# GpSimd sums the attention weights of a query tile before TensorE adds them over the keys

## The reference

```python
s = jnp.einsum('bhtd,bhsd->bhts', q, k) * w_intra
num = w_inter[..., None] * jnp.einsum('bhvk,bhtk->bhtv', C, q) + jnp.einsum('bhts,bhsv->bhtv', s, v)
den = w_inter * jnp.einsum('bhk,bhtk->bht', n, q) + jnp.sum(s, axis=-1)
h = num / jnp.maximum(jnp.abs(den), jnp.exp(-m_t))[..., None]
```

## Time and profile before

| | us |
|---|---|
| median of 3 runs | 1104.81 (1104.47 to 1109.66) |
| profiled execution | 1102.33 |
| its span | 1100.6 |
| VectorE busy | 452.7 |
| ScalarE busy | 254.4 |
| GpSimd busy | 155.4 |

### The profile page before, as it was taken

The page is one execution under the profiler, slowest core; times in us unless marked ns, Lnnn a source line. Parts: engine busy times, 40 slices in busy tenths (PEclk is TensorE's granted clock), DMA queues, the critical chain, the costliest instruction groups (busy, mean ns, idle before and its releaser), DMA issues.

```text
span 1100.6 us, 12588 instructions
## 1 busy us (share of the span) xinstructions
PE 1077.2 (98%) x4688; PEld 702.4 (64%) x4688; DVE 452.7 (41%) x1075; ACT 254.4 (23%) x525; POOL 155.4 (14%) x240
## 2 busy tenths in 40 slices
PE   7999999999999999999999999999999999999997
PEld 5777777777765354453634677777766666656667
DVE  7433243333347577575665100005243333343215
ACT  3211111111235323232331000010123333242221
POOL 5200010000110324113232011011110101000100
PEclk9999999999999999999999999999999999999999
DMA  6323223322346997979979322122211101202202
GB/s 256 106 82 130 86 81 129 128 81 106 111 144 248 337 372 286 339 278 354 368 303 329 151 75 76 38 77 99 87 54 45 60 20 60 94 17 101 72 24 97
DMA packets 44637, 162.26 MB, mean 147 GB/s; under 512 B 4844, under 2 KB 9196, under 8 KB 35632
## 3 DMA queue, kind: packets, MB, share of 16 engines
q1 hardware_dynamic: 44592, 161.65, 40.5%
HBM read 104.42 MB, written 57.21 MB: 147 GB/s over the span
## 4 chain that ended last, share of the span: by engine, by line
PE 91%; DVE 5%; DMA 2%; ACT 1%; issue 1%; POOL 0%; SPq 0%; DVEq 0%; ACTq 0%; POOLq 0%
PE work_b L633 27%; PE work_a L633 23%; PE work_b L1077 5%; PE work_a L896 5%; PE work_a L790 4%; PE bank L681 3%; PE bank L863 2%; PE work_b L846 2%; DVE arena L1890 2%; PE work_a L1147 2%; PE bank L1122 2%; PE bank L1252 1%; PE work_a L1107 1%; PE work_a L872 1%; PE bank L1125 1%; PE work_a L1220 1%
## 5 line engine op out<-in xcount | busy, mean ns | idle before, releaser
L633 PE MATMUL work_b<-arena,ring 128*128 128x320 f32 x832 | 230.5, 433 | 0.0
L633 PEld LDWEIGHTS work_b<-arena,ring 128*128 128x128 f32 x832 | 155.6, 190 | 61.0
L633 PE MATMUL work_a<-arena,ring 128*128 128x320 f32 x640 | 177.7, 436 | 6.7 <-DMA ring<-in_stream 6.7
L633 PEld LDWEIGHTS work_a<-arena,ring 128*128 128x128 f32 x640 | 121.6, 192 | 55.7 <-DMA ring<-in_stream 6.7
L1890 DVE SCALAR_TENSOR_TENSOR arena<-arena,bank 128x512 f32<-128x512 f32 x128 | 87.1, 743 | 65.1 <-PE bank L863 65.1
L1711 DVE COPY arena<-bank 128x384 f32<-128x384 f32 x64 | 28.5, 486 | 130.1 <-PE bank L681 130.0
L633 PE MATMUL work_a<-xc,ring 128*128 128x320 f32 x256 | 70.4, 434 | 1.9 <-ACT arena L1423 1.3
L633 PE MATMUL work_b<-xc,ring 128*128 128x320 f32 x256 | 69.6, 432 | 0.0
L896 PE MATMUL work_a<-arena 128*128 128x512 f32 x128 | 64.4, 615 | 2.8 <-ACT arena L1405 2.8
L633 PEld LDWEIGHTS work_a<-xc,ring 128*128 128x128 f32 x256 | 48.3, 190 | 23.6 <-ACT arena L1423 2.1
L633 PEld LDWEIGHTS work_b<-xc,ring 128*128 128x128 f32 x256 | 48.6, 190 | 20.3
(11 more groups left out here) (289 smaller groups left out, 1342.2 us busy)
## 6 DMA issues: line engine op xcount, KB each, us to landing
ring<-in_stream SPq DMA_DIRECT2D x66, 512.0 KB, 3.5
arena<-in_c SPq DMA_DIRECT2D x32, 1024.0 KB, 8.2
out_s_c<-arena SPq DMA_DIRECT2D x32, 1024.0 KB, 5.6
v_scratch<-arena SPq DMA_DIRECT2D x16, 320.0 KB, 4.7
k_scratch<-arena SPq DMA_DIRECT2D x16, 320.0 KB, 4.4
z_scratch<-arena SPq DMA_DIRECT2D x16, 320.0 KB, 4.6
arena<-k_scratch SPq DMA_DIRECT2D x4, 1280.0 KB, 12.9
arena<-z_scratch SPq DMA_DIRECT2D x4, 1280.0 KB, 9.8
```

The source lines that it names most:

```text
L633: done = mm(halves(buf)[:, a, :], lhs, rhs[:, a * HALF:(a + 1) * HALF], start=first, stop=last)
```

## The change

A new SBUF buffer ptsum of 512 columns holds the sums over key tiles. Behind the product of key tile s (s = 1 to 3), GpSimd adds tile s of pt to what it has for the query tiles s to 3: first tile 0 plus tile 1 (384 columns), then plus tile 2 (256), then plus tile 3 (128). After the addition s, the block of query tile s is complete. It waits for the addition before, and for VectorE's product, and raises weights_summed. The three additions stand at the head of GpSimd's work for a head, ahead of inverse_root(h, 0).

TensorE's sums are then one matmul for each query tile: tile 0 straight from pt, tiles 1 to 3 from ptsum, and the streams' as before. All five stand in small_sums, in each head; the scores have none between them any more. The semaphore's declaration is left out here.

```diff
--- before.py
+++ after.py
...
@@ -310,6 +310,7 @@
         hn = [take(HD) for _ in range(2)]
         cps = [take(HD) for _ in range(2)]
         kwsum = take(KH, P)
+        ptsum = take(SEQ)
         st6, mv = take(TT, 6), take(TT, 2)
         tiny = take(TT, 8)
         den_s = take(16)
@@ -768,9 +769,9 @@
             def weights_of(s, t):
                 return pt[:, OFF[s] + (t - s) * P:OFF[s] + (t - s + 1) * P]
 
-            def key_sum(s, t):
-                mm(small[:, S_DEN + t:S_DEN + t + 1], weights_of(s, t), ones_f[:, 0:1],
-                   start=s == keys_of(t)[0], stop=s == keys_of(t)[-1], skip_group_check=True)
+            def key_sum(t):
+                lhs = ptsum[:, t * P:(t + 1) * P] if 0 < t < NP else weights_of(t, t)
+                return mm(small[:, S_DEN + t:S_DEN + t + 1], lhs, ones_f[:, 0:1], start=True, stop=True, skip_group_check=True)
 
             def old_sum(h, q):
                 return mm(small[:, S_NQ:S_NQ + STREAMS], q_t[:, q, :], n_t[:, h, q, :],
@@ -793,22 +794,19 @@
                         last.then_inc(score_mm, 1)
                     if t == 0:
                         old_sum(h, q)
-                    elif h and t >= 2 and t - 2 + q < NP:
-                        key_sum(t - 2, t - 2 + q)
 
             def small_sums(h):
                 if h == 0:
                     pe.wait_ge(bc_out, 1)
                     pe.wait_ge(G.bfree[0], c.all(G.bfree[0], ahead=1))
                     pe.wait_ge(cols_ready, 4)
-                    for s in range(NP - 1):
-                        pe.wait_ge(score_out, s + 1)
-                        for t in range(s, NP):
-                            key_sum(s, t)
+                pe.wait_ge(score_out, TT * h + 1)
+                key_sum(0)
+                for t in range(1, NP):
+                    pe.wait_ge(weights_summed, (NP - 1) * h + t)
+                    key_sum(t)
                 pe.wait_ge(score_out, TT * (h + 1))
-                key_sum(NP - 1, NP - 1)
-                mm(small[:, S_DEN + NP:S_DEN + NP + 1], weights_of(NP, NP), ones_f[:, 0:1],
-                   start=True, stop=True, skip_group_check=True).then_inc(small_mm, 1)
+                key_sum(NP).then_inc(small_mm, 1)
 
             project_head(0)
             for t in range(2):
@@ -2216,7 +2214,19 @@
 
             head_basis(0)
             scratch_written(pool)
+            def sum_weights(h):
+                if h:
+                    pool.wait_ge(small_mm, 2 * h)
+                for s in range(1, NP):
+                    if s > 1:
+                        pool.wait_ge(weights_summed, (NP - 1) * h + s - 1)
+                    pool.wait_ge(score_out, TT * h + s + 1)
+                    first = pt if s == 1 else ptsum
+                    op = g.tensor_tensor(ptsum[:, s * P:SEQ], first[:, s * P:SEQ], pt[:, OFF[s]:OFF[s] + WID[s]], ALU.add)
+                    op.then_inc(weights_summed, 1)
+
             for h in range(HEADS):
+                sum_weights(h)
                 inverse_root(h, 0)
                 inverse_root(h, 1)
                 if h:
```

More of the change, by code:

```diff
@@ L246, in program @@
             out_squared out_summed prompt_root sample_squared sample_root y_sample
-            bc_mm bc_out proj_mm q_out k_kept exp_ready score_mm score_out small_mm small_out upd_mm upd_done pv_mm norm_done turn_mm turn_out pc_mm pc_out y_added""".split()
+            bc_mm bc_out proj_mm q_out k_kept exp_ready score_mm score_out small_mm small_out upd_mm upd_done pv_mm norm_done turn_mm turn_out pc_mm pc_out y_added weights_summed""".split()
         (const_in, ones_ready, squares, root, normed, tap0, conv_done, xcs_ready, xc_kept, tail_kept,
@@ L257, in program @@
          bc_mm, bc_out, proj_mm, q_out, k_kept, exp_ready, score_mm, score_out, small_mm, small_out, upd_mm, upd_done,
-         pv_mm, norm_done, turn_mm, turn_out, pc_mm, pc_out, y_added) = (sem(n) for n in names)
+         pv_mm, norm_done, turn_mm, turn_out, pc_mm, pc_out, y_added, weights_summed) = (sem(n) for n in names)
         x_in = [sem(f"x_in{n}") for n in range(4)]
```

## The result

The changed kernel takes 1097.31 us (median of 7 runs, 1096.91 to 1099.55) against 1104.04 us of the kernel before, measured beside it (7 runs, 1102.95 to 1109.66): a ratio of 0.9937, 95% interval 0.9919 to 0.9956. That is 6.7 us less, a change of 0.6%, while the forecast had 2.9. The profiled execution took 1097.53 us, span 1095.8, so between the two profiled executions only 4.8 us are gone. The experiments had to explain two things: this gap between 4.8 and 6.7, and why even the 4.8 is more than the 2.9 forecast.

The account below looks back on a forecast made before the run. TensorE, busy for 98% of the span, was taken as the bound. 3 x (-1.38) for heads 1 to 3 plus 1.2 in head 0 gave -2.9 us, so a median of 1101.9 us (-0.26%), range 1098.3 to 1106.2.

Parts of the forecast that it names:

- Price of a sum: One one-column matmul on TensorE, among scores or in small_sums: 0.23 us, with 0.21 and 0.24 as ends.
- Heads 1 to 3: Seams: nine sums leave the scores, three join small_sums, GpSimd's chain ends in time; gain of 1.38 us per head.
- rival C: Slower: the chain of additions becomes the bound of every seam, 0.9 us lost per head; 1109.5 us, chance 0.07.
- Head 0: Sums there wait for GpSimd's additions, delayed by VectorE through the lock; loss of 1.2 us, ends 0.4 and 1.7.
- The other engines follow TensorE's clock, so the gain is kept: Rest of the kernel: keys, transfers and GpSimd's queue delay nothing, so 1.38 us per head stays won.
- It is 2.5 us below the median of the runs shown: Profiled execution 1102.33 us against median 1104.81; the same -2.9 us was applied to the median, giving 1101.9.
- B: Gain goes into a new wait for delayed additions: heads gain 0.3 us, head 0 loses 1.7; 1105.6 us, chance 0.20.
- A: Full gain: sums were the limit, head 0 gains too, 24 matmuls less save 5.5 us; 1099.3 us, chance 0.13.

Follow-up runs that it names:

- no_additions: Changed kernel without GpSimd's additions and the waits for them, each sum taking only its own tile's block; 1097.08 us, ratio 0.9923 to the kernel before.
- long_chain: Changed kernel with one more GpSimd addition of 512 columns ahead of the three in each head; 1102.69 us, ratio 0.9986 to the kernel before.
- masks_late: Changed kernel with VectorE's masked queries of head 0 (two SBUF operands) moved behind the copy of the sums; 1097.99 us, ratio 0.9938 to the kernel before.
- padded: Changed kernel with seven more one-column matmuls in small_sums of heads 1 to 3; 1107.79 us, ratio 1.0031 to the kernel before.
- sums_moved: Kernel before with all ten sums of each head in small_sums, none between the scores, nothing on GpSimd; 1107.55 us, ratio 1.0032 to the kernel before.
- old_head0: Changed kernel, but head 0 keeps its eleven one-column matmuls without additions; 1098.28 us, ratio 0.9935 to the kernel before.
- head0_only: Kernel before with the change in head 0 only, old sums in heads 1 to 3; 1103.99 us, ratio 0.9993 to the kernel before.

## Why the prediction was right or wrong

The change was forecast too small: 1101.9 against 1097.31 measured, 1.0 us below the end of the range, and "no change" was given 0.82 where the measured 0.6% lies just past its bound of 0.5%. The mechanism in the seams and in head 0 was right. Two steps failed: the one that carried the gain unchanged through the rest of the kernel, and the one that carried it from the profiled execution to the median.

**Price of a sum, right.** 0.23 us was taken. Scores and turn of a seam shrank from 414.90 - 406.17 = 8.73 to 414.00 - 407.39 = 6.61 us, 2.12 (2.07 forecast). Back to back a sum takes 0.208.

**Heads 1 to 3, mechanism right, size 0.17 short in each.** 1.55 us instead of 1.38. The three more sums cost 1.04 - 0.46 = 0.58 us and not 0.69, and of the 2.12 about 0.12 is not the nine sums: in before the first sum starts 0.55 us behind the start of the turn, at 414.90, where VectorE's last product had just ended, and in the changed kernel, where it needs only tile 0's, 0.43 us behind it (414.00 - 413.57).

```profile
414.35 0.60 PE L881 MATMUL bank<-ident,arena 128*128 128x128 f32 x4
```

No wait for GpSimd, no harm from the additions (no_additions), and a margin of 0.10 us against 0.13: the chain of GpSimd was worked out to 0.1 us from neighbours' rows. long_chain shows that behind this margin nearly every further microsecond is paid for; with a period of 66.05, still below 66.65, it does not reach the point of rival C.

**Head 0, mechanism right.** 0.89 us lost (1.2 forecast, within 0.4 to 1.7). The lock between GpSimd and VectorE makes the additions 2.72 - 2.34 = 0.38 us longer (masks_late), so at most that much of the loss is the lock's; the rest is that the additions can't start before the product of tile 1. The wait that was forecast before the fourth sum (1.5 to 3 us) came before the second, third and fourth, 1.76 us together.

**"The other engines follow TensorE's clock, so the gain is kept", wrong.** This step failed first. It asked of the transfers only whether they would come too late after the change, and not which of them TensorE was already waiting for. The chain of waits of before held the answer: its DMA share of 2% was the first load of the input (6.30 us) and one transfer of 10.46 us out of ScalarE's buffer, with 1.31 us of idle TensorE at its end. I put a uniform shift on it. The wait vanished with the shorter period, worth 1.4 us in the profiled execution and about 1.6 in the mean of before's three traces (1.45 at the end and 0.18 at head 3). That it goes with the period is shown (padded has it back); why a shorter period lets the store land in time stays open.

**"It is 2.5 us below the median of the runs shown", taken as a constant, wrong.** This step failed second. The profiled execution of before was one without low clock in the heads; its other two traces are longer because TensorE runs at half clock for 3.4 and 6.8 us in head 0. That surplus isn't the same for both kernels. The means of the three traces of before against the two of the changed kernel (without the runs with other buffers), from the broadcast to the output projection, are 254.35 and 247.30 us: 7.05 less, which is the size of the medians' 6.7. By parts: seams 3 x 1.55 = 4.65; head 0 at full clock -0.89; store waits 1.6; low clock in before's traces, (2.44 + 0.89 + 1.64) / 3 = 1.66. Together 7.0. All executions taken together point to the same size: their mean clock is 0.9963 over the 85 of before beside the experiments and 0.9978 over 13 of the changed kernel, and over those 85 the time rises by about 1.0 us for each 0.001 of clock, which gives an estimate of 1.5 us for the clock.

Why the changed kernel suffers less from the low clock is shown in one part: its waits in head 0 cover one low stretch among the scores (10.17 against 11.24 us). It also has less of it (none in its two traces, some in two of the three of before), and the cause of that stays open. The rows of sums in head 0 would fit what padded and sums_moved show. Against them speak old_head0, which keeps the eleven sums there and had a mean clock of 0.9977 in 6 executions, head0_only, which has the five and had 0.9963 in 12, and long_chain and padded, which have a low stretch in head 0 behind five sums with waits between them. The higher clock goes with the change in heads 1 to 3, yet no trace of before has a low clock in its seams.

**Rivals.** B and C didn't happen. A, the full gain of 5.5 us, came nearest in time (1099.3) and for a wrong reason: head 0 gained nothing, and what made up for it were the store's wait and the clock.

No version tried is better than the changed kernel beyond the uncertainty.

## What to carry to other kernels

Before pricing a change, list the waits of the bounding engine itself, however small, and ask of each whether a shorter loop would remove it; a uniform shift is a claim that has to be shown. Look at the clock of every execution, and not only of the profiled one: if the profiled one lies below the median, the surplus is a mechanism of its own and can change with the edit. And eleven or twelve one-column matmuls in a row were dear twice here, 0.2 us each and the clock behind them; spread among full matmuls they cost only themselves.

## What the runs showed of the hardware

TensorE's granted clock fell to one half (1.2 GHz) for 3.4 us although TensorE was busy without a gap, behind a row of eleven or twelve matmuls with one moving column (2.4 to 2.6 us of them). In padded it did so in two of three seams, in sums_moved in three of three, and these kernels were 0.3% slower than before where the work alone would have them equal or faster. In no other of the seventeen traces is the clock low in a seam. In head 0 it fell in thirteen of the seventeen, for 3.4 to 6.8 us at a time.

GpSimd's addition and a VectorE instruction with two SBUF operands held each other up in both directions: VectorE's 0.42 us instruction took 1.00 behind a running addition of 384 columns, and GpSimd's 0.46 us addition took 0.78 beside VectorE's products of 512 columns.
